# Dispatch table of a mixture-of-experts block: a product of two one-hot tables in place of indirect stores to DRAM

## The reference

```python
eid = gi[:, None] * EXPERTS_PER_GROUP + ik          # (512, top): experts chosen by each token
flat_e = eid.reshape(-1)
order = jnp.argsort(flat_e)                         # token-expert pairs sorted by expert
counts = jnp.zeros((N_EXPERTS,), jnp.int32).at[flat_e].add(1)
padded = (counts + BLOCK - 1) // BLOCK * BLOCK      # each expert starts on a fresh block
dest = start_pad[se] + jnp.arange(n) - start_raw[se]
buf_tok = jnp.full((cap,), t).at[dest].set(flat_tok[order])   # slot -> token
xb = h_pad[buf_tok]                                 # rows gathered for the experts
```

## Time and profile before

| what | value |
|---|---|
| median of 3 runs | 4770.29 us (4761.27, 4770.29, 4772.77) |
| profiled execution, its own time | 4766.14 us |
| its span | 4764.3 us |
| PE busy | 3619.7 us (76%) |
| DVE busy | 1288.0 us (27%) |
| POOL busy | 888.8 us (19%) |
| mean granted TensorE clock | 0.866 of full speed |
| DMA queue q1 | 763.14 MB, 42.8% of 16 engines |

### The profile page before, as it was taken

One profiled execution on the slowest core, in us unless ns is written; L12 is line 12 of the kernel. 1 busy time (PEld: TensorE's weight loads), 2 busy tenths in 40 slices (PEclk: granted clock), 3 DMA queues, 4 the chain that ended last, 5 costly groups with the idle time before them and its releaser, 6 DMA issues. The chain is left out here.

```text
span 4764.3 us, 54180 instructions
## 1 busy us (share of the span) xinstructions
PE 3619.7 (76%) x18771; PEld 2098.0 (44%) x18772; DVE 1288.0 (27%) x2211; ACT 802.4 (17%) x1548; POOL 888.8 (19%) x923
## 2 busy tenths in 40 slices
PE   4989998998658887797488775976688528888881
PEld 2468966894323332333233222432444315555541
DVE  2533453443310001312100003036453321111115
ACT  1422242221011111100011111110132001111110
POOL 0034403440021111000211110033100032222223
PEclk7988998999779898897799897977689769999996
DMA  6840000002169999332599995320010129997895
GB/s 242 204 109 1 1 36 19 1 1 89 60 271 407 404 394 365 142 120 112 222 388 386 409 378 214 119 86 0 12 54 25 55 87 329 336 321 281 296 336 177
DMA packets 217938, 891.91 MB, mean 187 GB/s; under 512 B 57096, under 2 KB 57994, under 8 KB 183883
## 3 DMA queue, kind: packets, MB, share of 16 engines
q1 hardware_dynamic: 164812, 763.14, 42.8%
q10 hardware_dynamic: 30628, 76.61, 4.5%
q0 software_dynamic: 22368, 50.39, 3.4%
HBM read 831.01 MB, written 78.46 MB: 191 GB/s over the span
## 5 line engine op out<-in xcount | busy, mean ns | idle before, releaser
L1586 PE MATMUL ps<-weight_ring,moe_xT 128*64 128x256 f32 (+1 forms) x1344 | 441.0, 483 | 71.0 <-DMA weight_ring<-in_w_dram 45.1
L1586 PE MATMUL ps<-moe_spare,moe_xT 128*64 128x256 f32 (+1 forms) x1280 | 429.5, 491 | 64.1 <-issue 64.1
L1588 PE MATMUL ps<-weight_ring,moe_xT 128*64 128x256 f32 (+1 forms) x1344 | 441.4, 483 | 0.0
L1588 PE MATMUL ps<-moe_spare,moe_xT 128*64 128x256 f32 (+1 forms) x1280 | 430.4, 491 | 0.0
L1560 POOL COPY moe_xg<-moe_xin 64x1024 f32<-64x1024 f32 x168 | 173.5, 1033 | 1287.0 <-PE ps L1574 674.6
L1669 DVE TENSOR_TENSOR moe_act<-moe_sg,ps 64x256 f32<-64x256 f32 (+1 forms) x164 | 87.2, 532 | 973.2 <-ACT moe_sg L1647 973.2
L1586 PEld LDWEIGHTS ps<-weight_ring,moe_xT 128*64 128x64 f32 x1344 | 186.5, 141 | 302.5 <-issue 209.7
L1586 PEld LDWEIGHTS ps<-moe_spare,moe_xT 128*64 128x64 f32 x1280 | 179.7, 143 | 289.4 <-issue 260.0
L1672 DVE COPY moe_y<-ps 128x512 f32 x164 | 113.4, 691 | 688.0 <-PE ps L1605 503.8
L1605 PE MATMUL ps<-moe_spare,moe_aT 128*64 128x512 f32 x904 | 236.8, 660 | 25.2 <-issue 16.1
L1605 PE MATMUL ps<-weight_ring,moe_aT 128*64 128x512 f32 x944 | 232.9, 626 | 25.3 <-issue 16.6
(11 more groups left out here) (559 smaller groups left out, 5873.7 us busy)
## 6 DMA issues: line engine op xcount, KB each, us to landing
weight_ring<-in_w_dram SPq DMA_DIRECT2D x96, 2048.0 KB
moe_spare<-in_w_dram SPq DMA_DIRECT2D x96, 2048.0 KB
weight_ring<-in_w_exp_gu_dram SPq DMA_DIRECT2D x32, 2048.0 KB
moe_spare<-in_w_exp_gu_dram SPq DMA_DIRECT2D x32, 2048.0 KB
expert_rows<-moe_y ACTq DMA_DIRECT2D x328, 128.0 KB
weight_ring<-in_w_exp_dn_dram SPq DMA_DIRECT2D x16, 2048.0 KB
moe_spare<-in_w_exp_dn_dram SPq DMA_DIRECT2D x16, 2048.0 KB
expert_rows<-delta_o SPq DMA_DIRECT2D x1, 24320.0 KB, 126.5
```

Of the source, the lines that this page charges most:

```text
L1586: nc.tensor.matmul(m.ps[0:UR, 0, 0:F], xT[:, k, :], gate[:, k, :], start=(k == 0), stop=(k == KD - 1))
L1588: last = nc.tensor.matmul(m.ps[UR:P, 0, 0:F], xT[:, k, :], up[:, k, :], start=(k == 0), stop=(k == KD - 1))
```

## The change

The three constants of the dispatch are kept in SBUF by the caller and loaded by SP in the routing stage: the triangle `earlier`, the token numbers `ids` (now minus EMPTY, 4096), and a new table `consts` with the rows 0,1,2,... and 0,64,128,.... SP waits for them at the end of its list in that stage.

In the dispatch nothing goes through DRAM any more. The `nth` chain stands ahead of the wait for PE. All choices are handled by one instruction over [tiles, choices, experts]. The slot number is split into its unit (times 64) and its row, and for each tile DVE compares both against the constant rows: `row_hot` [choices, 64] and `unit_hot` [choices, units]. POOL multiplies `row_hot` with the token number. PE then adds up the products of `row_hot` and `unit_hot`, even choices into partitions 0 to 63 and odd ones into 64 to 127. DVE adds the two halves and EMPTY.

```diff
@@ both routing stages @@
             sp.dma_start(rw[:, :, 4:36], router_e.rearrange("(k p) n -> p k n", p=P)).then_inc(s.in_, 16)
+            for dst, src in consts:
+                sp.dma_start(dst, src).then_inc(s.consts_in, 16)
             m.ring.stream(sp, after)
+            sp.wait_ge(s.consts_in, 16 * len(consts))
@@ dispatch_stage @@
         def _(sp):
-            sp.dma_start(ids[:], m.ids).then_inc(s.ids_in, 16)
-            sp.dma_start(earlier[:], m.earlier).then_inc(s.earlier_in, 16)
-            sp.wait_ge(s.empty, 1)
-            rows = table.rearrange("(u s) o -> u (s o)", s=UR)
-            sp.dma_start(rows, tab[0:units + 1, 0, :]).then_inc(s.filled, 16)
             m.ring.stream(sp, after)
-            sp.wait_ge(s.scattered, 16 * NT * top)
-            sp.dma_start(tab[0:units + 1, 1, :], rows).then_inc(s.read_back, 16)
-            sp.wait_ge(s.read_back, 16)
...
-            pe.wait_ge(s.read_back, 16)
-            nc.tensor.transpose(m.ps[0:UR, 2, 0:units + 1], tab[0:units + 1, 1, :],
-                                m.ident[0:units + 1, 0:units + 1]).then_inc(s.turned, 1)
+            for t in range(NT):
+                pe.wait_ge(s.row_hot, t + 1)
+                pe.wait_ge(s.unit_hot, t + 1)
+                for k in range(top):
+                    last = nc.tensor.matmul(m.ps[UR * (k % 2):UR * (k % 2) + UR, 2, 0:UN], row_hot[:, t, k, :],
+                                            unit_hot[:, t, k, :], start=(t == 0 and k < 2),
+                                            stop=(t == NT - 1 and k >= top - 2))
+            last.then_inc(s.turned, 1)
...
-            nc.vector.memset(tab[:, 0, :], float(EMPTY)).then_inc(s.empty, 1)
+            nc.vector.memset(none[:], float(EMPTY)).then_inc(s.blank, 1)
+            x, y, d = nth[:, 0], nth[:, 1], 1
+            link(nc.vector.tensor_copy(x, sel))
+            while d < E:
...
+            link(nc.vector.tensor_tensor(x, x, sel, ALU.mult))
+            which = steps[:, 1:top + 1].unsqueeze(1).unsqueeze(3).to_broadcast([P, NT, top, E])
+            link(nc.vector.tensor_tensor(pick[:], by_choice(x), which, ALU.is_equal))
...
+            link(nc.vector.memset(cnt[:], 0.0))
             dve.wait_ge(s.ranks, 1)
...
-            for k in range(top):
-                link(nc.vector.tensor_scalar(pick[:], x, float(k + 1), None, ALU.is_equal))
-                link(nc.vector.tensor_tensor(pick2[:], pick[:], rank[:], ALU.mult))
-                link(nc.vector.tensor_reduce(destf[:, :, k], pick2[:], AX_X, ALU.add))
-                nc.vector.tensor_copy(r.dest[:, :, k], destf[:, :, k]).then_inc(s.dest, 1)
-                link(nc.vector.tensor_tensor(pick[:], pick[:], wt, ALU.mult))
-                link(nc.vector.tensor_reduce(r.share[:, :, k], pick[:], AX_X, ALU.add))
+            link(nc.vector.tensor_tensor(pick2[:], pick[:], by_choice(rank[:]), ALU.mult))
+            link(nc.vector.tensor_reduce(destf[:], pick2[:], AX_X, ALU.add))
+            link(nc.vector.tensor_scalar(unit[:], destf[:], 1.0 / UR, 0.5 / UR - 0.5, ALU.mult, ALU.add))
+            link(nc.vector.tensor_scalar(unit[:], unit[:], 1.5 * 2 ** 23, None, ALU.add))
+            link(nc.vector.tensor_scalar(unit[:], unit[:], -1.5 * 2 ** 23, float(UR), ALU.add, ALU.mult))
+            link(nc.vector.tensor_tensor(row[:], destf[:], unit[:], ALU.subtract))
+            for t in range(NT):
+                hot = row_hot[:, t]
+                nc.vector.tensor_tensor(hot, steps[:, 0:UR].unsqueeze(1).to_broadcast([P, top, UR]),
+                                        row[:, t, :].unsqueeze(2).to_broadcast([P, top, UR]),
+                                        ALU.is_equal).then_inc(s.row_there, 1)
+                nc.vector.tensor_tensor(unit_hot[:, t], sixty_fours[:, 0:UN].unsqueeze(1).to_broadcast([P, top, UN]),
+                                        unit[:, t, :].unsqueeze(2).to_broadcast([P, top, UN]),
+                                        ALU.is_equal).then_inc(s.unit_hot, 1)
+            link(nc.vector.tensor_copy(r.dest[:], destf[:]))
+            link(nc.vector.tensor_tensor(pick[:], pick[:], by_choice(wt), ALU.mult))
+            link(nc.vector.tensor_reduce(r.share[:], pick[:], AX_X, ALU.add))
...
+            link(nc.vector.tensor_copy(r.slot_token[:, UN:UN + 3], none[:]))
             dve.wait_ge(s.turned, 1)
+            link(nc.vector.tensor_scalar(half[:, 0, :], m.ps[0:UR, 2, 0:UN], float(EMPTY), None, ALU.add))
+            link(nc.vector.tensor_copy(half[:, 1, :], m.ps[UR:P, 2, 0:UN]))
+            link(nc.vector.tensor_tensor(half[:, 0, :], half[:, 0, :], half[:, 1, :], ALU.add))
+            nc.vector.tensor_copy(r.slot_token[:, 0:UN], half[:, 0, :]).then_inc(s.done, 1)
...
         def _(pool):
-            pool.wait_ge(s.ids_in, 16)
-            pool.wait_ge(s.filled, 16)
-            for k in range(top):
-                pool.wait_ge(s.dest, k + 1)
-                for t in range(NT):
-                    nc.gpsimd.indirect_dma_start(
-                        out=table, out_offset=bass.IndirectOffsetOnAxis(ap=r.dest[:, t, k:k + 1], axis=0),
-                        in_=ids[:, t:t + 1], in_offset=None).then_inc(s.scattered, 16)
-            pool.wait_ge(s.scattered, 16 * NT * top)
+            for t in range(NT):
+                pool.wait_ge(s.row_there, t + 1)
+                nc.gpsimd.tensor_scalar(row_hot[:, t], row_hot[:, t], r.ids[:, t:t + 1], None,
+                                        ALU.mult).then_inc(s.row_hot, 1)
```

More of the change, by code:

```diff
@@ L1225, in rank_in_eights, with route_groups_stage @@
     link(nc.vector.tensor_reduce(rank, gt, AX_X, ALU.add))
-def route_groups_stage(m, tag, hT, router_g, router_e, wt, sel, after):
+def route_groups_stage(m, tag, hT, router_g, router_e, wt, sel, after, consts):
     nc = m.nc
@@ L1239, in route_groups_stage @@
     c = st.sb("cols", [P, 6, NT])
-    s = st.sem("in_ logits chain groups_shifted groups_exp shifted exp")
+    s = st.sem("in_ logits chain groups_shifted groups_exp shifted exp consts_in")
     with st.block() as block:
@@ L1300, in route_groups_stage, with route_sigmoid_stage @@
     st.close()
-def route_sigmoid_stage(m, tag, hT, router, bias, wt, sel, after):
+def route_sigmoid_stage(m, tag, hT, router, bias, wt, sel, after, consts):
     nc = m.nc
@@ L1318, in route_sigmoid_stage @@
     c = st.sb("cols", [P, NT])
-    s = st.sem("in_ logits chain scores")
+    s = st.sem("in_ logits chain scores consts_in")
     with st.block() as block:
@@ L1377, in dispatch_stage @@
     E = n_exp
+    UN = units + 1
     rank = st.sb("rank", [P, NT, E])
@@ L1380, in dispatch_stage @@
     nth = st.sb("nth", [P, 2, NT, E])
-    pick = st.sb("pick", [P, NT, E])
-    pick2 = st.sb("pick2", [P, NT, E])
+    pick = st.sb("pick", [P, NT, top, E])
+    pick2 = st.sb("pick2", [P, NT, top, E])
     destf = st.sb("destf", [P, NT, top])
-    tab = st.sb("table", [P, 2, UR])
-    ids = st.sb("ids", [P, NT])
-    earlier = st.sb("earlier", [P, P])
-    table = nc.dram_tensor(f"slot_table{tag}", [(units + 1) * UR, 1], F32).ap()
-    s = st.sem("ids_in earlier_in empty filled ranks chain dest scattered read_back turned done")
+    row = st.sb("row", [P, NT, top])
+    unit = st.sb("unit", [P, NT, top])
+    row_hot = st.sb("row_hot", [P, NT, top, UR])
+    unit_hot = st.sb("unit_hot", [P, NT, top, UN])
+    half = st.sb("half", [UR, 2, UN])
+    none = st.sb("none", [UR, 3])
+    steps, sixty_fours = r.consts[:, 0, :], r.consts[:, 1, :]
+    s = st.sem("blank ranks chain row_there row_hot unit_hot turned share done")
     with st.block() as block:
@@ L1409, in _ @@
                     nc.tensor.matmul(out, m.ones, sel[:, b, :], start=(b == 0), stop=False)
-                nc.tensor.matmul(out, earlier[:], sel[:, t, :], start=(t == 0), stop=True)
+                nc.tensor.matmul(out, r.earlier[:], sel[:, t, :], start=(t == 0), stop=True)
             for t in range(NT):
@@ L2758, in build @@
         m.earlier = a["c_base"][:, 2, :]
-        m.before, m.ids = m.beforeb[:, :], a["c_ids"]
+        m.before, m.ids, m.steps = m.beforeb[:, :], a["c_ids"], a["c_steps"]
         at = plan_weights(m, a)
@@ L2935, in host_constants @@
     return {"c_base": base_masks(), "c_before": np.tile(before, (P, 1)), "c_delta": delta_masks(),
-            "c_ids": np.arange(T, dtype=np.float32).reshape(NT, P).T.copy(), "c_mix": mix_masks()[0]}
+            "c_ids": np.arange(T, dtype=np.float32).reshape(NT, P).T - np.float32(EMPTY),
+            "c_steps": np.tile(np.stack([np.arange(P), UR * np.arange(P)]).astype(np.float32), (P, 1, 1)), "c_mix": mix_masks()[0]}
 def kernel(**inputs):
```

24 lines of the change are left out of this document (11 added, 13 removed).

## The result

| | before | changed kernel |
|---|---|---|
| median | 4765.78 us (4 runs, 4753.76 to 4772.77) | 4681.75 us (4 runs, 4678.39 to 4685.10) |
| profiled execution, its span | 4766.14, 4764.3 us | 4679.94, 4678.1 us |
| DVE from first to last instruction of the dispatch, layers 0, 1, 2 | 33.82, 34.79, 81.76 us | 17.45, 17.45, 33.40 us |
| the same, forecast | | 17.7, 17.7, 34.3 us |

What follows compares the result with a forecast made beforehand. Each dispatch was taken as one long chain on the path, 150.4 us together, waiting on DRAM. Savings of 16.1, 17.1 and 47.5 us, sum 80.7, off the mean 4768.1 gave 4687 us, range 4674 to 4705.

Steps and rivals of the forecast that it cites:

- Start and ranks: Dispatch start: without SP's loads PE starts with the stage and finishes the ranks at 6.3 us in all three layers.
- The moved chain: `nth` chain ahead of the wait for PE: ends at 3.9 us in layers 0 and 1, hidden; 7.3 in layer 2.
- Counting: DVE's counting in the dispatch, L1427 to L1443: 4.85 us, 5.88 in layer 2, to 11.2 and 13.1.
- Slot numbers: DVE's product and reduction over all choices plus four tiny operations: to 12.9 us, in layer 2 to 18.65.
- End: Four small instructions closing the dispatch: 0.94 and 1.2 us, so dispatches end at 17.7, 17.7 and 34.3 us.
- One-hot tables: DVE's two comparisons per tile plus POOL's multiply (0.25 and 0.6 us), one at a time: 2.6 us, 9.4 in layer 2.
- Products: PE's table products hide behind DVE's tail, except at the upper end in layer 2, adding about 1.5 us.
- Routing: Three more loads in the routing stage cost nothing; competition with routing weights may cost 0.5 us each.
- Rival B: POOL not let in while DVE has instructions ready, so multiplies start late: saves 67 to 74 us; 11%.
- Rival C: POOL's first multiply needs code loaded, costing 5 to 10 us in layer 0: 4692 to 4697 us; 9%.
- Rival D: Experts do not move along with the shorter dispatch, and all is given back: 4768 us; 3%.
- Rival E: POOL pays for each of six switches between arithmetic and indirect DMAs; at 16 us each, 4783 us; 3%.

Runs made afterwards that it cites:

- e8: The changed kernel with the `nth` chain and the first comparison back behind the counting; 4696.22 us.
- e3: The kernel before, with only `ids` and `earlier` loaded in the routing stage; 4737.0 us, ratio to before 0.9963.
- e4: The changed kernel with DVE waiting after each row comparison until POOL has multiplied; 4686.6 us.
- e9: The changed kernel with the share product and reduction moved from the dispatch to the start of the expert stage; 4662.98 us.
- e10: e9 with comparison and multiply fused on DVE, without POOL, in layers 0 and 1, layer 2 unchanged; 4677.3 us, ratio to before 0.9825.

## Why the prediction was right

The median is 4681.75 us against a forecast of 4687 and a range of 4674 to 4705; the dispatches gave 82.1 us where the sum said 80.7. The other 4 us by which the median lies under the forecast are less than the rest of the span moves by itself. Step by step, in us from DVE's first instruction in the stage:

| point | layer 0: forecast, measured | layer 2: forecast, measured |
|---|---|---|
| counting starts (L1441) | 6.3, 6.24 | 7.3, 7.28 |
| slot numbers start (L1454) | 11.2, 11.11 | 13.1, 13.16 |
| tables start (L1463) | 12.9, 12.85 | 18.65, 18.69 |
| tables done (L1469) | 15.4, 14.56 | 28.05, 26.88 |
| halves start (L1475) | 16.8, 16.55 | 33.1, 32.22 |
| end | 17.7, 17.45 | 34.3, 33.40 |

- *Start and ranks, The moved chain, Counting, Slot numbers* and *End* came out within 0.1 us a step. In layers 0 and 1 PE's ranks hide the chain (2.43 us of idle DVE), in layer 2 the chain itself is the bound; e8 confirms both sizes. *Start and ranks* said that PE would be done at 6.3 us in all three. In layer 2 it was done at 4.4 (3774.0), with a granted clock of 0.73 on the way. That was harmless, since DVE came later anyway; in e3, where it is not hidden, it gave 2 us more than expected. The price of an operation on two tensors of 2048 elements was read from a reduction of one tensor; the product took the same 2.29 us (L1454), so this did no harm.
- *One-hot tables* had two wrong numbers that nearly cancelled, by luck. It priced the multiply by the copy, at 0.25 and 0.6 us, with twice that as its bound; it is 0.61 and 1.56 (e4), beyond the bound. It charged DVE with the whole of it, reading as one at a time, and DVE loses only a part: 0.4 of 1.56 us in layer 2, and some 0.2 us over all four tiles in layer 0, where a tile takes 0.43 us and not 0.64. A tile in layer 2 was forecast at 2.35 us and takes 2.15; the first, which is not stretched, takes 1.74. With the right price and the same reading of the earlier trace rows the tables of layer 2 would have been forecast at 4 x 3.31 = 13.2 us; the forecast was 9.4, and they took 8.2. The trace of before could have told more of both. POOL has a multiply by a column there, of the same 512 elements, at 1.04 us, a nearer row than the copy though still short of 1.56:

```profile
L1008 POOL TENSOR_TENSOR x_resident<-v,delta_beta 128x512 f32<-128x512 f32 x12 | 12.5, 1039 | 0.1
```

  And the hold-up in the earlier trace rows stands in another place than it was read: DVE's 1280 elements in 1.57 us are 0.1 over the prediction's own line and not 0.2, while the 1408 elements before them took 3.63 us where the line gives 1.6. DVE's next operation of this line (L2153) shows the same, 5.67 us where the line gives 1.5, beside a POOL operation on two tensors:

```profile
3228.36 5.63 POOL L2127 TENSOR_TENSOR x_resident<-x_resident,mix_hq 128x2048 f32<-128x2048 f32 x1
3229.67 5.67 DVE L2153 TENSOR_TENSOR hgprep_pair<-hgprep_wq,mix_hk 128x1280 f32<-128x1280 f32 x1
```

  So DVE can lose most of a POOL instruction's time, and in the change it lost a quarter. What makes the difference no run here has tried.
- *Products* said that DVE's tail covers them. In layer 2 it does, with 2.7 us to spare (e9 takes 2.6 of them back); the tail itself took 5.34 us and not 5.05, since its product ran beside POOL's last multiply (2.58 us instead of 2.29). In layers 0 and 1 it does not: DVE waits 0.52 us, because POOL's four multiplies, 2.69 us in all, run past DVE's comparisons. This 0.5 us was hidden in the total by the 0.8 us that the tables took less than forecast. Both ends of the step's range for the last tile of layer 2, 1.7 to 3.5 us, are for the lower clock; PE's last two groups went at the higher one, in 1.09 us each.
- *Routing* at nothing: the routing of layer 0, from its first load to the dispatch, took 31.5 us in both executions of before and 31.6 to 31.8 in the nine with the new dispatch; the routing of layer 2 took 91.4 and 91.7 us against 91.6 to 92.2, and that of layer 1 scatters by 1.5 us. So a cost of some tenths each is likely, within the 0.5 that the prediction allowed.
- Rival B falls: POOL got in while DVE had instructions ready, and PE had two of its four groups in layer 2 under way before DVE's list of tables ended. Rival C falls: PE is released 14.13 us after the start in layer 0 as in layer 1, POOL's first multiply takes 0.84 us in both, and it started 0.1 us after the first row table was there (1312.52, 1312.62). The 6 us which the Trainium skill gives in "GPSIMD Engine Reference", section 2.1, Instruction dispatch, for a first call of freshly loaded code, were not paid on the path in this case; the configuration instruction ran at 1299.33, with 13.3 us ahead of the multiply in which POOL had nothing to do, so these runs don't show whether something was paid there unseen. Rival D falls: the expert loads go out 0.94 to 0.97 us after each dispatch, and the rest of the span has not grown by anything like the 82 us that would be given back. Rival E falls: the first gather of layer 0 starts 3.93 us after the stage's start, against 3.88 before (3.67 against 3.65 in the other two), as the timeline of layer 0 shows:

```profile
1317.79 1.80 POOL L1551 MEMSET moe_xin<- 64x2048 f32 x1 [2.49 <-POOLq L184]
...
1321.72 1.15 POOL L1560 DMA_INDIRECT moe_xin<-hidden,moe_icol  x1 [0.94 <-POOL moe_icol L1556]
```

What stays open: why the experts of layer 0 take a little longer now. PE's last product of that stage came 534.2, 534.6 and 533.0 us after its start in the three executions with the old dispatch (before twice, and e3), and 535.7 to 540.4 in the nine with the new one. All nine lie above all three, by some 3 us in the mean, so a small part of the gain in the dispatch is probably given back there. Layers 1 and 2 show no such parting, the total can't tell 3 us, and no run looked for the cause.

## What to carry to other kernels

When a stage is one chain with every engine mostly idle, write down its critical list with the start time of every step; here that gave each step without POOL in it to 0.1 us, and the one left to an analogy was the one that was off. A second engine that takes work off the first need not be fast, but it must be done when the first looks: POOL is two to three times slower than DVE at this multiply (0.61 against 0.29 us, 1.56 against 0.49) and still worth lending it, as long as the other way is a separate multiply on DVE; in layers 0 and 1 the fused comparison without POOL was 0.4 us shorter once the shares were moved (e10 against e9). And before work is moved out of a stage, look at what the waiting engine would wait for next: the same move (e9) was worth 2.6 us in layer 2 and nothing in the others.
